# First pair of conv-norm statistics as split products behind the output products, with a new order table

## The chip, the cores and the metric

The kernel runs on one core of a Trainium2 chip. The metric is the time of one execution on the device in microseconds. TensorE is called PE here, VectorE DVE, ScalarE ACT, GpSimd POOL, and SyncE (which issues most transfers) SP. The trace is that of one profiled execution; its times count from the start of its span.

## The reference

One decoder layer over 2048 positions of width 1024: RMS norm, one input projection, a gated linear attention (GLA) on four heads, beside it a convolution of width 31 on 512 channels with a group norm, one output projection, and a feed-forward part with squared ReLU.

```python
xn = rmsnorm(h, norm1_g[l])
proj = jnp.einsum('bsd,de->bse', xn, w_in[l])
...
o_gla = gla_chunked(q, k, v, log_a)
o_gla = rmsnorm(o_gla, gla_norm_g[l]).reshape(B, S, GLA_VAL) * jax.nn.silu(g)
...
u = c_in * jax.nn.sigmoid(c_gate)
u = causal_depthwise_conv(u, conv_w[l], conv_b[l])
o_conv = jax.nn.silu(channel_group_norm(u, conv_norm_g[l], conv_norm_b[l]))
mixed = jnp.concatenate([o_gla, o_conv], axis=-1)
h = h + jnp.einsum('bse,ed->bsd', mixed, w_out[l])
...
ff = jnp.square(jax.nn.relu(jnp.einsum('bsd,df->bsf', hn, w_mlp_in[l])))
h = h + jnp.einsum('bsf,fd->bsd', ff, w_mlp_out[l])
```

The change concerns `channel_group_norm`: mean and variance over groups of 64 channels at each position, then scale, gain and silu.

## The kernel before

The mixer works through four blocks of 512 positions (b = 0 to 3 in the code, blocks one to four in the text), the feed-forward part follows. Channels lie on the partitions, 128 at a time; the 512 convolution channels are four tiles j = 0 to 3, handled in two pairs. Nearly every matrix product is done in fp32 precision as three products of rounded parts (`three_products`, lines 83 to 85: high by high, high by low, low by high). A half column of the input projection is four such triples, 12 products of 128x128 by 128x512.

The convolution runs on DVE. A tap (L1724) adds one shifted and weighted copy of `u_sb` to a sum in PSUM; 31 taps make a tile, and the last tap of a tile writes the result to `y_sb`. `("taps", p, i, n)` in the table is n taps of pair p from the i-th of 62 on.

The group norm of a pair goes through the steps `cn_mean` (PE forms the group means as a product with the block matrix `mean_grp`, DVE subtracts them from `y_sb` at L2216, ACT squares), `cn_var` (PE forms the group means of the squares, ACT takes the logarithm), `cn_rstd` (ACT exponential, POOL multiplies), `cn_silu` and `cn_mixed` (ACT and POOL write the rounded part `mix_hi` and the rest `mix_lo`, which the output products read). The sums come in two forms. A plain one is a single fp32 product (L2586 for means, L2596 for variances). A split one (`mean_of`, L2271 and L2272) is two products of rounded operands, the high and the low part of the data with `mean_grp_r`; for it ACT first writes the rounded copy or square to `mix_hi` (L1615, L1606) and POOL the difference to `mix_lo` (L1169, L1179). Step `cn_split` is that preparation for the mean; for the variance it is part of `cn_mean`. Before the change the first pair (tiles 0 and 1) has plain sums in all blocks, the second pair split ones. The rows of `mix_hi` and `mix_lo` that hold split data are the ones from which the output products of the block before read, so ACT waits for those products to end first (`w_used`, `OUT_END`).

GLA goes in four chunks of 128 positions per block. For a chunk, PE forms scores in two steps (`gla_scores c 0` and `1`; L2618, L2625; the transposes L2633 of `k_end` close the first, and they wait for the state of the chunk before), DVE picks the valid ones into `probs` by masked copies (`gla_select`; L2055, L2065, L2075, L2198), PE forms the chunk's output (L2654, L2658) and DVE updates the state (`state`, L2209). POOL makes the decayed keys (`gla_decayed`), ACT the exponentials, DVE the exponents (`gla_expo`; L2175 to L2177, subtractions with both operands in SBUF).

The order of everything in the mixer is the table `ORDER`, a list of (block, step, arguments) made ahead of time by a planner. Each engine runs through this one list and does its own part of each step in that sequence, so the table fixes the order on each engine and nothing else; waits on semaphores keep data right. In the table the entries of output products `out` in block b belong to the output of block b-1. The function `cn_bank` says into which PSUM bank a sum goes.

## Time and profile before

| | us |
|---|---|
| median of 3 runs | 2024.85 |
| lowest and highest | 2024.81, 2025.76 |
| the profiled execution | 2024.25 |
| its span in the trace | 2022.2 |
| PE busy in the span | 2000.1 |
| DVE, ACT, POOL busy | 1473.9, 956.6, 445.9 |

The span is the time from the first to the last instruction that the profiler recorded; 2.05 us of the execution lie around it. The mixer takes some 780 us of it, the feed-forward part the rest. A busy share is the mean over parts with different limits, so the stretches and the waits have to be read too. Matmuls overlap in the trace: a product of 128x512 is shown as 0.39 us long while the next begins 0.23 us after it, so distances between starts are what a product costs.

### The profile page before, as it was taken

To read this page: it belongs to the slowest core of one execution; us is meant where nothing else is said; L and a number is where in the kernel's file an instruction comes from. 1 tells how busy PE (TensorE), PEld (TensorE's weight loads), DVE (VectorE), ACT (ScalarE), POOL (GpSimd) and SP (SyncE) were. 2 spreads that over 40 slices of the span, in tenths; PEclk is the share of its full clock that TensorE was granted. 3 is DMA by queue.
4 is the path that set the end of the run, shared out by engine and by line. 5 is a ranking of instruction groups with operands and counts; after the bars stand their busy time and mean duration, and the time that the engine had idled before them with its cause. 6 is when DMAs were issued, how large, how long until landed. Compare 5 with 4: busy or idle time off the path is not lost.

```text
span 2022.2 us, 27147 instructions
## 1 busy us (share of the span) xinstructions
PE 2000.1 (99%) x9898; PEld 1635.4 (81%) x9898; DVE 1473.9 (73%) x2178; ACT 956.6 (47%) x1361; POOL 445.9 (22%) x593
## 2 busy tenths in 40 slices
PE   8999999999999999999999999999999999999998
PEld 7787778787877778888888888888888888888887
DVE  3899978887878978877789777777664646545475
ACT  4456664355244563565557645554332333323253
POOL 5553475235126441000000000000020201202031
PEclk9999999999999999999999999999999999999999
DMA  6884458555555555444445433335967557565674
GB/s 227 285 289 152 139 202 295 167 168 186 198 200 191 179 208 191 162 146 144 148 163 206 153 122 127 126 121 197 376 231 266 188 203 265 181 220 185 206 239 177
DMA packets 175268, 395.76 MB, mean 196 GB/s; under 512 B 15424, under 2 KB 64672, under 8 KB 174624
## 3 DMA queue, kind: packets, MB, share of 16 engines
q1 hardware_dynamic: 154688, 317.47, 46.3%
q10 hardware_dynamic: 20448, 76.56, 10.8%
q8 instruction: 79, 1.29, 0.3%
q14 instruction: 53, 0.43, 0.1%
HBM read 301.70 MB, written 92.27 MB: 195 GB/s over the span
## 4 chain that ended last, share of the span: by engine, by line
PE 90%; DVE 6%; issue 2%; ACT 2%; POOL 0%; DMA 0%; DVEq 0%; ACTq 0%; POOLq 0%
PE acc L83 24%; PE acc L85 24%; PE acc L84 24%; PE acc L2565 3%; PE acc L2566 3%; PE acc L2567 3%; DVE acc L1724 2%; PE acc L2625 1%; PE acc L2520 1%; PE acc L2519 1%; PE acc L2521 1%; PE acc L2284 1%; ACT ring_hi L1355 1%; PE acc L2658 1%; DVE ring_sum L1869 1%
## 5 line engine op out<-in xcount | busy, mean ns | idle before, releaser
L1986 DVE TENSOR_TENSOR down_lo<-down_raw,down_hi 128x1536 fp32r<-128x1536 f32 x112 | 200.5, 1790 | 231.1 <-ACT down_hi L1441 231.1
L84 PE MATMUL acc<-down_lo,down_hi 128*128 128x512 f32 x896 | 348.5, 389 | 0.0
L83 PE MATMUL acc<-down_hi 128*128 128x512 f32 x896 | 348.5, 389 | 0.0
L85 PE MATMUL acc<-down_hi,down_lo 128*128 128x512 f32 x896 | 348.5, 389 | 0.0
L1441 ACT ACTIVATE down_hi<-down_raw 128x1536 fp32r<-128x1536 f32 x112 | 166.7, 1488 | 360.8 <-PE acc L85 192.9
L1724 DVE SCALAR_TENSOR_TENSOR acc<-u_sb,cw_col,acc 128x512 f32<-128x512 f32 x464 | 312.9, 747 | 0.3
L1355 ACT ACTIVATE ring_hi<-ring_sum 128x512 fp32r<-128x512 f32 x155 | 97.8, 631 | 250.3 <-DVE ring_sum L1869 247.9
L83 PE MATMUL acc<-xT_hi,wt 128*128 128x512 f32 x512 | 203.6, 398 | 0.7 <-ACT q_sb L1534 0.7
L1100 POOL TENSOR_TENSOR rows_a<-rows_a,second 128x512 f32<-128x512 f32 x20 | 25.3, 1296 | 803.6 <-ACT second L1449 655.5
L84 PE MATMUL acc<-xT_lo,wt 128*128 128x512 f32 x512 | 199.5, 390 | 0.0
L85 PE MATMUL acc<-xT_hi,wt 128*128 128x512 f32 x512 | 199.5, 390 | 0.0
L84 PEld LDWEIGHTS acc<-down_lo,down_hi 128*128 128x128 f32 x896 | 168.2, 188 | 35.0
L85 PEld LDWEIGHTS acc<-down_hi,down_lo 128*128 128x128 f32 x896 | 168.2, 188 | 34.9
L83 PEld LDWEIGHTS acc<-down_hi 128*128 128x128 f32 x896 | 168.2, 188 | 34.9
L1869 DVE TENSOR_TENSOR ring_sum<-raw_w 128x512 f32<-128x512 f32 x155 | 108.1, 698 | 66.3 <-PE acc L85 64.8
L83 PE MATMUL acc<-mul_hi,ring_hi 128*128 128x512 f32 x372 | 145.5, 391 | 0.4 <-issue 0.4
L85 PE MATMUL acc<-mul_hi,ring_lo 128*128 128x512 f32 x372 | 144.8, 389 | 0.0
L84 PE MATMUL acc<-mul_lo,ring_hi 128*128 128x512 f32 x372 | 144.8, 389 | 0.0
L1878 DVE TENSOR_TENSOR ring_lo<-ring_sum,ring_hi 128x512 fp32r<-128x512 f32 x155 | 107.2, 692 | 18.4 <-ACT ring_hi L1355 3.8
L83 PEld LDWEIGHTS acc<-xT_hi,wt 128*128 128x128 f32 x512 | 96.2, 188 | 23.2 <-issue 2.2
L85 PEld LDWEIGHTS acc<-xT_hi,wt 128*128 128x128 f32 x512 | 96.1, 188 | 20.6
L84 PEld LDWEIGHTS acc<-xT_lo,wt 128*128 128x128 f32 x512 | 96.2, 188 | 20.5 <-issue 1.2
(304 smaller groups left out, 4113.2 us busy)
## 6 DMA issues: line engine op xcount, KB each, us to landing
wt<-w_kept SPq DMA_DIRECT2D x168, 512.0 KB, 3.3
down_raw<-f_kept ACTq DMA_DIRECT2D x109, 512.0 KB, 4.3
raw_w<-in_w_mlp_in SPq DMA_DIRECT2D x32, 1024.0 KB, 5.9
f_kept<-f_tile SPq DMA_DIRECT2D x128, 256.0 KB, 2.0
down_raw<-in_w_mlp_out SPq DMA_DIRECT2D x64, 512.0 KB, 3.6
w_kept<-wt SPq DMA_DIRECT2D x48, 512.0 KB, 5.3
down_raw<-in_w_mlp_out SPq DMA_DIRECT2D x64, 256.0 KB, 3.2
down_more<-f_kept ACTq DMA_DIRECT2D x29, 512.0 KB, 5.3
```

Source lines behind the costliest of these rows:

```text
L83: nc.tensor.matmul(out, w_hi, x_hi, start=first, stop=False, skip_group_check=onto)
L84: nc.tensor.matmul(out, w_hi, x_lo, start=False, stop=False, skip_group_check=onto)
L85: return nc.tensor.matmul(out, w_lo, x_hi, start=False, stop=last, skip_group_check=onto)
L1355: nc.scalar.activation(blocks(ring_hi[:, j % RING, :]), src, ACT.Copy).then_inc(a_hi, 1)
L1441: nc.scalar.activation(down_hi[d % RING][:, :], down_raw[d % DOWN_RAW][:, 512:2048], ACT.Copy).then_inc(d_hi, 1)
L1724: nc.vector.scalar_tensor_tensor(out=y_sb[:, j, :] if k == TAPS - 1 else bank, in0=u_sb[:, j, k:k + BLK], scalar=cw_col[:, j, k:k + 1], in ...
L1869: nc.vector.tensor_tensor(blocks(ring_sum[:, j % RING, :]), w1_block(w, a), w1_block(w, b), op).then_inc(a_sum, 1)
L1878: nc.vector.tensor_tensor(blocks(ring_lo[:, slot, :]), src, blocks(ring_hi[:, slot, :].bitcast(F32)), ALU.subtract).then_inc(a_lo, 1)
L1986: nc.vector.tensor_tensor(down_lo[slot][:, :], down_raw[d % DOWN_RAW][:, 512:], down_hi[slot][:, :].bitcast(F32), ALU.subtract).then_inc(d ...
L2565: nc.tensor.matmul(out, mix_hi[:, k, c], w_hi[:, slot, :], start=(k == 0), stop=False)
L2566: nc.tensor.matmul(out, mix_hi[:, k, c], w_lo[:, slot, :], start=False, stop=False)
L2567: ins = nc.tensor.matmul(out, mix_lo[:, k, c], w_hi[:, slot, :], start=False, stop=(k == KT - 1))
```

## The change

For the first pair in blocks one to three, mean and variance become split sums like those of the second pair. ACT's rounded copies and squares and POOL's differences come on, in steps `(b, cn_split, 0)` and `(b, cn_mean, 0)`. Since they use the rows of `mix_hi` and `mix_lo`, `cn_mean 0` of blocks two and three now stands behind the output products of the block before (it waits for `sum_ok`) and uses banks 4 and 5; ACT waits only for the first pair's taps. Block four keeps its plain first pair. The count of split parts gets a function of its own, `nth_part`, and one wait of a residual load and one of the output are kept for the last block alone. The table `ORDER` is made anew throughout, with the planner told of a mutual exclusion of DVE and POOL in SBUF; `make_wz`, which splits a small weight, is now its first entry.

```diff
@@ -92,152 +92,161 @@
-    (-1, "make_masks", 0), (0, "x_load", 0), (-1, "conv_gate_a", 0), (-1, "make_masks", 1), (-1, "conv_gate", 0),
...
+    (-1, "make_wz"), (-1, "make_masks", 0), (0, "x_load", 0), (-1, "conv_gate_a", 0), (-1, "conv_gate", 0),
...
@@ -625,9 +634,19 @@
 
         def cn_bank(b, j):
 
-            if b == NB - 1 and j >= 2:
-                return Y_BANK[j % 2]
-            return j if j < 2 and not first(b) else 4 + j % 2
+            if b == NB - 1:
+                return j if j < 2 else Y_BANK[j % 2]
+            return 4 + j % 2
+
+        def in_parts(b, step):
+
+            return b < NB - 1 or step[1] == 1
+
+        def nth_part(b, name, j):
+
+            if b == NB - 1:
+                return b * 2 * CT + (2 if name == "cn_mean" else 0) + j - 2 + 1
+            return (b * 2 + j // 2) * CT + (2 if name == "cn_mean" else 0) + j % 2 + 1
 
         def pair(step):
 
@@ -794,7 +813,8 @@
                 elif half == 0:
 
                     sp.wait_ge(cn_f, (m + 1) * CT)
-                    sp.wait_ge(cn_n, (m + 1) * CT + 2)
+                    if m + 1 == NB - 1:
+                        sp.wait_ge(cn_n, (m + 1) * CT + 2)
                 else:
                     sp.wait_ge(h_st, (m * 2 + half + 1) * 16)
                 sp.dma_start(res(m, half)[:, :, :], tok(x_t, m, half)).then_inc(res_ld[half], 16)
@@ -1165,7 +1185,7 @@
                     pass
                 elif name == "cn_split" and b < NB - 1:
                     for j in pair(step):
-                        pool.wait_ge(cn_part_hi, b * CT + j - 1)
+                        pool.wait_ge(cn_part_hi, nth_part(b, name, j))
                         nc.gpsimd.tensor_tensor(mix_lo[:, HEADS + j, :], y_sb[:, j, :],
                                                 mix_hi[:, HEADS + j, :].bitcast(F32), ALU.subtract).then_inc(cn_part_lo, 1)
                 elif name == "gn_square" and b < NB - 1:
@@ -1173,9 +1193,9 @@
                         pool.wait_ge(gn_sq, 2 * (b * HEADS + h + 1))
                         nc.gpsimd.tensor_tensor(mix_lo[:, h, :], gn_r[:, h, :], mix_hi[:, h, :].bitcast(F32),
                                                 ALU.subtract).then_inc(gn_sq_lo, 1)
-                elif name == "cn_mean" and step[1] == 1 and b < NB - 1:
+                elif name == "cn_mean" and b < NB - 1:
                     for j in pair(step):
-                        pool.wait_ge(cn_part_hi, b * CT + j + 1)
+                        pool.wait_ge(cn_part_hi, nth_part(b, name, j))
                         nc.gpsimd.tensor_tensor(mix_lo[:, HEADS + j, :], cn_work(j),
                                                 mix_hi[:, HEADS + j, :].bitcast(F32), ALU.subtract).then_inc(cn_part_lo, 1)
                 elif name == "cn_rstd":
@@ -1597,12 +1617,14 @@
                 elif name == "cn_mean":
                     if first(b) and step[1] == 0:
                         act.wait_ge(xt_pe, 2 * 2 * TT)
-                    if b - 2 + step[1] >= 0:
-                        act.wait_ge(h_st, ((b - 1 + step[1]) * 2 + 1) * 16)
+                    if b == NB - 1 and step[1] == 0:
+                        act.wait_ge(h_st, ((b - 1) * 2 + 1) * 16)
+                    elif not first(b):
+                        act.wait_ge(h_st, (b * 2 + 1) * 16)
                     for j in pair(step):
                         act.wait_ge(cn_dev, b * CT + j + 1)
                         nc.scalar.activation(cn_work(j), y_sb[:, j, :], ACT.Square).then_inc(cn_sq, 1)
-                        if step[1] == 1:
+                        if in_parts(b, step):
                             nc.scalar.activation(mix_hi[:, HEADS + j, :], y_sb[:, j, :],
                                                  ACT.Square).then_inc(cn_part_hi, 1)
                 elif name == "cn_split":
@@ -1610,7 +1632,7 @@
                         act.wait_ge(w_used, base(b) + OUT_END)
                     else:
                         act.wait_ge(v_st, 2 * KT * 16)
-                    act.wait_ge(tap_ok, (b + 1) * ALL_TAPS)
+                    act.wait_ge(tap_ok, b * ALL_TAPS + (step[1] + 1) * PAIR_TAPS)
                     for j in pair(step):
                         nc.scalar.activation(mix_hi[:, HEADS + j, :], y_sb[:, j, :], ACT.Copy).then_inc(cn_part_hi, 1)
                 elif name == "cn_var":
@@ -2216,12 +2238,12 @@
                         nc.vector.tensor_tensor(y_sb[:, j, :], y_sb[:, j, :], acc[:, cn_bank(b, j), :],
                                                 ALU.subtract).then_inc(cn_dev, 1)
                     for j in pair(step) if b == NB - 1 and step[1] == 1 else ():
-                        dve.wait_ge(cn_part_hi, b * CT + j + 1)
+                        dve.wait_ge(cn_part_hi, nth_part(b, name, j))
                         nc.vector.tensor_tensor(mix_lo[:, HEADS + j, :], cn_work(j),
                                                 mix_hi[:, HEADS + j, :].bitcast(F32), ALU.subtract).then_inc(cn_part_lo, 1)
                 elif name == "cn_split" and b == NB - 1:
                     for j in pair(step):
-                        dve.wait_ge(cn_part_hi, b * CT + j - 1)
+                        dve.wait_ge(cn_part_hi, nth_part(b, name, j))
                         nc.vector.tensor_tensor(mix_lo[:, HEADS + j, :], y_sb[:, j, :],
                                                 mix_hi[:, HEADS + j, :].bitcast(F32), ALU.subtract).then_inc(cn_part_lo, 1)
                 elif b == NB - 1 and name in ("cn_rstd", "cn_mixed") and step[1] == 1:
@@ -2291,7 +2313,7 @@
                     pe.wait_ge(*((sum_ok, (NB - 1) * LOWS) if t == 0 else (low_ok, m * LOWS + 2 * t)))
                 elif t == 0 and not first(m):
                     pe.wait_ge(v_ok, m * TT)
-                    if m > 1:
+                    if m == NB:
                         pe.wait_ge(cn_ln, (m - 1) * CT + 2)
                 elif t == 1 and not first(m):
                     pe.wait_ge(silu_ok, m * HEADS)
@@ -2570,33 +2592,31 @@
                         elif k == KT - 1:
                             ins.then_inc(out_pe, 1)
                 elif name == "cn_mean":
-                    if step[1] == 0:
+                    if not in_parts(b, step):
                         pe.wait_ge(tap_ok, b * ALL_TAPS + PAIR_TAPS)
-                    if step[1] == 0 and not first(b):
                         pe.wait_ge(v_ok, (b + 1) * TT)
                     else:
                         if not first(b):
                             pe.wait_ge(sum_ok, b * LOWS)
-                        elif step[1] > 0:
+                        if step[1] > 0 and b < NB - 1:
                             pe.wait_ge(cn_ln, b * CT + 2)
-                        if b < NB - 1:
                             pe.wait_ge(u_ok, (b + 1) * 2 * CT + 2)
                     for j in pair(step):
-                        if step[1] == 0:
+                        if not in_parts(b, step):
                             nc.tensor.matmul(acc[:, cn_bank(b, j), :], mean_grp[:, :], y_sb[:, j, :], start=True,
                                              stop=True).then_inc(cn_mean_pe, 1)
                         else:
-                            pe.wait_ge(cn_part_lo, b * CT + j - 1)
+                            pe.wait_ge(cn_part_lo, nth_part(b, "cn_split", j))
                             mean_of(acc[:, cn_bank(b, j), :], mean_grp_r, HEADS + j).then_inc(cn_mean_pe, 1)
                 elif name == "cn_var":
                     pe.wait_ge(cn_dev, b * CT + 2 * step[1] + 2)
                     for j in pair(step):
-                        if step[1] == 0:
+                        if not in_parts(b, step):
                             pe.wait_ge(cn_sq, b * CT + j + 1)
                             nc.tensor.matmul(acc[:, cn_bank(b, j), :], mean_grp[:, :], cn_work(j), start=True,
                                              stop=True).then_inc(cn_var_pe, 1)
                         else:
-                            pe.wait_ge(cn_part_lo, b * CT + j + 1)
+                            pe.wait_ge(cn_part_lo, nth_part(b, "cn_mean", j))
                             mean_of(acc[:, cn_bank(b, j), :], mean_grp_r, HEADS + j).then_inc(cn_var_pe, 1)
                 elif name == "gla_scores":
                     c, part = step[1:]
```

On PE in block two, the first pair's mean before the change (rows of the trace's program, in sequence; `q_in` and `qe_head` are GLA operands). Before:

```order
L2618 MATMUL acc<-qe_head,ke 64x128 [waits gn_ln,o_ok,qe_ok]
L2618 MATMUL acc<-qe_head,ke 64x128
L2625 MATMUL acc<-qe_head,ke 64x64 x8
L2633 MATMUL acc<-ident,k_end 128x128 [waits state_ok]
L2633 MATMUL acc<-ident,k_end 128x128
L2586 MATMUL acc<-y_sb,mean_grp 128x512 [waits v_ok,tap_ok]
L2586 MATMUL acc<-y_sb,mean_grp 128x512
L83 MATMUL acc<-xT_hi,wt 128x512 [waits w_again2,v_ok]
```

and after, where the product ahead of it is the last one of the first conv_gate column (`sum_ok` counts the output tiles of the block before):

```order
L83 MATMUL acc<-xT_hi,wt 128x512
L84 MATMUL acc<-xT_lo,wt 128x512
L85 MATMUL acc<-xT_hi,wt 128x512
L2293 MATMUL acc<-mix_hi,mean_grp_r 128x512 [waits cn_part_lo,sum_ok]
L2294 MATMUL acc<-mix_lo,mean_grp_r 128x512
L2293 MATMUL acc<-mix_hi,mean_grp_r 128x512 [waits cn_part_lo]
L2294 MATMUL acc<-mix_lo,mean_grp_r 128x512
L83 MATMUL acc<-xT_hi,wt 128x512 [waits w_again2,sum_ok]
```

The mean went from a place among the first chunk's scores, ahead of the output products, to one behind them, and each of the two plain products became two rounded ones.

On DVE in block one, around the masked copies of the third chunk (`probs`). Before:

```order
L2055 COPY_PREDICATED probs<-lvl_mask,acc 128x4x64 [waits probs_ok,o_pe,score_pe]
L2065 COPY_PREDICATED probs<-lvl_mask,acc 128x8x32 [waits probs_ok]
L1724 SCALAR_TENSOR_TENSOR acc<-u_sb,cw_col,acc 128x512 [waits tap_ok]
L1724 SCALAR_TENSOR_TENSOR y_sb<-u_sb,cw_col,acc 128x512 [waits tap_ok] x2
L2065 COPY_PREDICATED probs<-lvl_mask,acc 128x16x16 [waits probs_ok,score_pe]
L2085 COPY u_sb<-u_sb 128x30 [waits tap_ok]
L2089 TENSOR_TENSOR u_sb<-acc,sig 128x512 [waits u_ok,csig_ok,w_used]
L1719 TENSOR_SCALAR acc<-u_sb,cw_col,cb_col 128x512 [waits tap_ok,u_ok] x2
```

and after:

```order
L1746 SCALAR_TENSOR_TENSOR y_sb<-u_sb,cw_col,acc 128x512 [waits tap_ok] x2
L2107 COPY u_sb<-u_sb 128x30 [waits tap_ok]
L2111 TENSOR_TENSOR u_sb<-acc,sig 128x512 [waits u_ok,csig_ok,w_used]
L2077 COPY_PREDICATED probs<-lvl_mask,acc 128x4x64 [waits probs_ok,o_pe,score_pe]
L2087 COPY_PREDICATED probs<-lvl_mask,acc 128x8x32 [waits probs_ok]
L2087 COPY_PREDICATED probs<-lvl_mask,acc 128x16x16 [waits probs_ok,score_pe]
L2197 TENSOR_TENSOR fac<-cum 128x2x64 [waits ke_ok]
```

The taps that end the second pair (`y_sb`) and the product that makes `u_sb` now stand ahead of the masked copies, and the third masked copy follows the second one directly.

On DVE in block one, from the third chunk's last masked copy to the state update behind its output. Before:

```order
L2198 COPY_PREDICATED probs<-ident,acc 128x512 [waits upd_pe,probs_ok]
L2216 TENSOR_TENSOR y_sb<-y_sb,acc 128x512 [waits cn_mean_pe] x2
L1724 SCALAR_TENSOR_TENSOR acc<-u_sb,cw_col,acc 128x512 [waits tap_ok] x10
L2101 TENSOR_TENSOR z_parts<-acc,z_parts 32x512 [waits z_ok]
L1724 SCALAR_TENSOR_TENSOR acc<-u_sb,cw_col,acc 128x512 [waits tap_ok] x6
L2209 SCALAR_TENSOR_TENSOR state<-state,decay,acc 64x128 [waits state_ok,o_ok,upd_pe]
L2209 SCALAR_TENSOR_TENSOR state<-state,decay,acc 64x128 x3
L2111 TENSOR_SCALAR cum<-acc,bg_col 128x512 [waits fac_ok,gate_act]
L2055 COPY_PREDICATED probs<-lvl_mask,acc 128x4x64 [waits probs_ok,o_pe,score_pe]
L2065 COPY_PREDICATED probs<-lvl_mask,acc 128x8x32 [waits probs_ok]
```

and after:

```order
L2220 COPY_PREDICATED probs<-ident,acc 128x512 [waits upd_pe,probs_ok]
L2107 COPY u_sb<-u_sb 128x30 [waits tap_ok]
L2111 TENSOR_TENSOR u_sb<-acc,sig 128x512 [waits u_ok,csig_ok,w_used]
L1741 TENSOR_SCALAR acc<-u_sb,cw_col,cb_col 128x512 [waits tap_ok,u_ok] x2
L1746 SCALAR_TENSOR_TENSOR acc<-u_sb,cw_col,acc 128x512 [waits tap_ok] x6
L2123 TENSOR_TENSOR z_parts<-acc,z_parts 32x512 [waits z_ok]
L2231 SCALAR_TENSOR_TENSOR state<-state,decay,acc 64x128 [waits state_ok,o_ok,upd_pe]
L2231 SCALAR_TENSOR_TENSOR state<-state,decay,acc 64x128 x3
L1746 SCALAR_TENSOR_TENSOR acc<-u_sb,cw_col,acc 128x512 [waits tap_ok] x8
L2077 COPY_PREDICATED probs<-lvl_mask,acc 128x4x64 [waits probs_ok,o_pe,score_pe]
```

Between the last copy and the state update there were 16 taps and the subtraction of two means; now there are the product for `u_sb`, the two first taps and six more.

## Rows read from the trace of the kernel before

**Rows 1.** Page, part 1: busy us (share of span) and instructions of engines.

```profile
PE 2000.1 (99%) x9898; PEld 1635.4 (81%) x9898; DVE 1473.9 (73%) x2178; ACT 956.6 (47%) x1361; POOL 445.9 (22%) x593
```

**Rows 2.** Stretches: window in us, its length, then as the header row says.

```profile
core 0: us, PE busy (x) PEld busy (x) DVE busy (x) ACT busy (x) POOL busy (x), PEclk, DMA share, GB/s
...
100.00:200.00 100.00, 97.91 (x621) 77.75 (x620) 95.55 (x201) 55.89 (x79) 44.60 (x74) 1.00 0.68 227
...
600.00:700.00 100.00, 97.78 (x578) 78.28 (x578) 86.31 (x180) 53.98 (x79) 47.56 (x73) 1.00 0.53 179
...
800.00:2022.00 1222.00, 1214.52 (x5388) 1005.12 (x5386) 825.02 (x991) 553.73 (x752) 93.86 (x96) 1.00 0.55 189
```

**Rows 3.** Waits of PE: what waited, for whom, us in total, times, longest.

```profile
PE acc L2625 <- DVE probs L2065: 1.8, 2, 1.3
...
PE acc L2654 <- DVE probs L2198: 1.2, 1, 1.2
PE acc L2633 <- DVE state L2209: 1.2, 1, 1.2
PE acc L2640 <- ACT k_endT L1586: 1.1, 1, 1.1
PE acc L2674 <- DVE state L2209: 1.0, 1, 1.0
```

**Rows 4.** Timeline of PE, a plain pair: start us, us, line, operation.

```profile
155.46 1.88 PE L2586 MATMUL acc<-y_sb,mean_grp 128*128 128x512 f32 x4
156.78 0.80 PE L83 MATMUL acc<-xT_hi,wt 128*128 128x512 f32 x1
157.42 0.39 PE L84 MATMUL acc<-xT_lo,wt 128*128 128x512 f32 x1
```

**Rows 5.** Timeline of PE, a split pair and the product behind it.

```profile
194.90 0.40 PE L2271 MATMUL acc<-mix_hi,mean_grp_r 128*128 128x512 f32 x1
...
195.84 0.39 PE L2486 MATMUL acc<-xT_hi,wz 128*32 128x512 f32 x1
```

**Rows 6.** Groups of PE by line: busy us, mean ns of one record.

```profile
L2596 PE MATMUL acc<-res_sb,mean_grp 128*128 128x512 f32 x16 | 7.7, 605 | 0.0
L2586 PE MATMUL acc<-y_sb,mean_grp 128*128 128x512 f32 x16 | 7.5, 592 | 0.0
```

**Rows 7.** Timeline of PE, block one: idle time before and who ended it.

```profile
187.33 1.15 PE L2625 MATMUL acc<-qe_head,ke 128*64 128x64 f32 x32 [1.29 <-DVE probs L2065]
...
212.17 0.44 PE L2633 MATMUL acc<-ident,k_end 128*128 128x128 f32 x2 [1.16 <-DVE state L2209]
...
214.30 0.51 PE L2625 MATMUL acc<-qe_head,ke 128*64 128x64 f32 x10 [0.51 <-DVE probs L2065]
```

**Rows 8.** Timeline of DVE at that first wait.

```profile
184.88 0.75 DVE L1724 SCALAR_TENSOR_TENSOR acc<-u_sb,cw_col,acc 128x512 f32<-128x512 f32 x1
185.53 1.40 DVE L1724 SCALAR_TENSOR_TENSOR y_sb<-u_sb,cw_col,acc 128x512 f32<-128x512 f32 x2
186.85 0.42 DVE L2065 COPY_PREDICATED probs<-lvl_mask,acc 128x256 f32<-128x256 int32 x1
```

**Rows 9.** Timeline of DVE at the second.

```profile
206.57 4.03 DVE L1724 SCALAR_TENSOR_TENSOR acc<-u_sb,cw_col,acc 128x512 f32<-128x512 f32 x6
210.63 1.48 DVE L2209 SCALAR_TENSOR_TENSOR state<-state,decay,acc 64x128 f32<-64x128 f32 x4
```

**Rows 10.** Timeline, block two: POOL, and DVE beside it.

```profile
265.22 2.60 POOL L1188 TENSOR_TENSOR mix_lo<-y_sb,mix_hi 128x512 fp32r<-128x512 f32 x2 [0.69 <-ACT mix_hi L1637]
...
266.59 1.38 DVE L2176 TENSOR_TENSOR fac<-cum 128x128 f32<-128x128 f32 x1
267.89 0.28 DVE L2175 TENSOR_TENSOR fac<-cum 128x128 f32<-128x128 f32 x1
```

**Rows 11.** One tile each: ns of one, least, median, most; first and last start.

```profile
L1615 ACT ACTIVATE mix_hi<-y_sb x8: 613/624/630, 187.0 to 734.9; 128x512 fp32r<-128x512 f32 x8
...
L1169 POOL TENSOR_TENSOR mix_lo<-y_sb,mix_hi x6: 1272/1292/1297, 187.7 to 567.8; 128x512 fp32r<-128x512 f32 x6
```

295 lines of the change are left out of this document (152 added, 143 removed).

## The prediction, made before the changed kernel ran

> **What bounds the kernel now.** I read the engines' busy times first [rows 1]. TensorE (PE) is busy for 2000.1 us of a span of 2022.2 us; VectorE (DVE) comes next with 1473.9 us, GpSimd (POOL) has 445.9 us. A busy PE is not a PE at its peak, so the second view is the one by stretches [rows 2]. From 800 us to the end, the feed-forward part that the change does not touch, PE is busy for 1214.5 of 1222 us at a granted clock of 1.00. Whatever the mixer (0 to some 780 us) saves on PE therefore moves the whole later part forward, microsecond for microsecond: nothing else there is near a limit (DVE 825.0, POOL 93.9 us). In the mixer PE is also nearly full (97.9 us of 100 in one stretch shown, 97.8 in another), but DVE is full beside it in the first block: 95.6 us of 100 between 100 and 200 us, against 86.3 between 600 and 700 us. So there are two currencies: PE's own work, which counts in full, and the short times in which PE waits for DVE or ScalarE (ACT). The third view, PE's waits [rows 3], says how large the second one is: the five longest lines that lie in the mixer hold 1.8, 1.2, 1.2, 1.1 and 1.0 us, 6.3 us together. That is all there is to win from a better order on these lines; the rest must come from PE's work.
>
> **What the change removes and adds on PE.** In blocks one to three (b = 0, 1, 2) two means and two variances per block were plain fp32 products. Each is one instruction that leaves two records in the trace, so the two sums of one step stand as x4. A pair of them begins at 155.46 us, and the second of the products behind it begins at 157.42 us [rows 4]. Products of this size begin 0.23 us apart (156.78 is the modelled start of the product in between, which overlaps the last plain one), so the pair took 157.42 - 155.46 - 0.23 = 1.73 us. The split form is two rounded products for each sum; its pair, four products, begins at 194.90 us and the next work begins at 195.84 us: 0.94 us [rows 5]. The difference is 0.79 us a pair. The trace groups count 16 and 16 records of plain products, 592 and 605 ns each [rows 6], which is four pairs of means and four of variances; the last block keeps its two, so six pairs change: 6 x 0.79 = **4.8 us less work on PE**. Bounds: if only the time up to the modelled start of the next product were the pair's own (156.78 - 155.46 = 1.32 us), it would be 6 x 0.38 = 2.3 us; by the busy times (4 x 0.6 against four products 0.23 apart plus a tail) it would be at most some 5.5 us. I take 4.8, since start to start is what the engine can't give away.
>
> **What it adds elsewhere.** ACT gets, per block, two copies and two squares with rounded output, 0.62 us for a copy [rows 11] and as much taken for a square: 12 instructions, 7.5 us, on an engine that is busy for 56 and 54 us of 100 in the mixer's stretches [rows 2]. POOL gets 12 subtractions of 1.29 us [rows 11], 15.5 us, and it is busy for 45 and 48 of 100. I cost both at nothing for the end time, as long as the sums are not asked for early. The cover is the distance in PE's order. The longest new chain is at block two: the ACT copy can start only when the last output product of the block before is done (it writes the rows of mix_hi that those products read), then 0.62 us ACT and 1.29 us POOL, 1.9 us to the first part and 3.2 us to the second. On PE, scores and two half columns of conv_gate (24 products, 5.4 us) stand between the last output product and the first sum. So the sum has its operands some 3 us early; in block three the distance is longer still. The variance chain (subtract on DVE 0.7, four squares on ACT 2.5, two subtractions on POOL 2.6, 5.8 us) has ten half columns of 2.7 us of PE work to cover it in block two, and three and a chunk's output, some 10 us, in block three. Behind the waiting POOL instructions stand the decayed keys of the fourth chunk; these wait for the third chunk's scores anyway, which PE reaches some 13 us after the sum. If that cover were gone, each sum would stop PE for up to 3 us.
>
> **What it moves.** The last taps of a block's first pair of channel tiles had to be done before the pair's mean, and in blocks two and three that mean came ahead of all output products. Now it comes behind them. DVE gets over 40 us more for those taps (16 half columns of output, 12 products 0.23 us apart each), and the new table uses this: work on which PE waits goes ahead of taps. The two places that the waits name are in block one [rows 7]. At 187.33 us the second scores of the third chunk had waited 1.29 us for a masked copy of DVE; DVE was still in the last three taps (184.88 and 185.53, ending at 186.9) and reached the copy at 186.85 [rows 8]. In the new order this copy stands directly behind the first two, with no tap between. At 212.17 us the transposes of the fourth chunk had waited 1.16 us for the state of the third, which DVE began at 210.63 after six taps that began at 206.57 [rows 9], and the scores behind them another 0.51 us. PE had 12 products between the chunk's output and those scores; now it has 24 and the variance's four, 3.6 us more. These three waits, 1.29 + 1.16 + 0.51 = 3.0 us, should go. What is late next? DVE is still the fuller engine in block one, and the table also rearranges the rest of it, which the trace of before can't show. I bound what new waits cost from below by nothing and from above by the lines of rows 3: as much as all that is there now, 6.3 us, once more. I take one new wait of the longest kind [rows 7], 1.3 us, since in blocks two to four DVE has more room than in block one [rows 2]. Net: 3.0 - 1.3 = **1.7 us less waiting**, with ends at 6.3 us less and 6.3 - 3.0 = 3.3 us more.
>
> **The sum.** The profiled execution took 2024.25 us (span 2022.2 and 2.05 around it); the median of three runs is 2024.85 us, 0.6 above it. 2024.25 - 4.8 - 1.7 = 2017.75 us, and with the 0.6 us the median comes to about **2018.4 us**.
>
> **A rule weighed.** While POOL ran two subtractions from 265.22 us on, a DVE subtraction with both inputs in SBUF, which takes 0.28 us elsewhere in its series, took 1.38 us and ended as POOL's second one ended [rows 10]. The Trainium skill (SBUF — State Buffer, "Who interferes with whom") says so too: a Vector instruction with two SBUF inputs and a GpSimd instruction that reads SBUF take one shared read interface in turn, and the later of the two is blocked for the whole of the other. By that rule, the trace agrees, the change is a risk: every added POOL instruction reads two SBUF tensors. It is the rival of the other side, below.
>
> **The rivals.** (1) *The order's waits don't shrink.* The old waits go and new ones of the same size or more take their place: PE's saving stands alone or is eaten. 2024.85 - 4.8 + 0 to 3.3 us = 2020.1 to 2023.4 us, with a tail beyond it if several new waits are longer than any of the old. For it: two tables made by a planner share hardly a place after the first block, and 6.3 us of waits were left by the last one. Against it: the two longest go by construction. (2) *DVE's relief reaches further.* All of the 6.3 us goes: 2024.85 - 4.8 - 6.3 = 2013.8 us. For it: later mean, fewer deadlines for taps in blocks two and three; against it: the waits at 1.2 us (chunk output), 1.1 (k_endT) and 1.0 (group norm) are on places that the change doesn't address [rows 3]. (3) *Slower: POOL holds DVE.* Each of the 12 new POOL subtractions can hold one DVE instruction with two SBUF inputs for 1.38 - 0.28 = 1.1 us [rows 10], 13.2 us in all; if all of it reached PE, 2024.85 - 4.8 + 13.2 = 2033.3 us. It ends slower than before by more than 0.2% from 8.9 us on, that is if at least 8 of the 12 fall on work that PE is about to ask for. Against it: most of DVE's instructions are taps, which read one SBUF and one PSUM operand and went on undisturbed, and the table was made knowing of it. (4) *It doesn't do what it says.* The plain pair's tail overlapped the products behind it, and only 2.3 us go: 2022.5 us with waits as they are.
>
> **How the numbers follow.** The forecast (2017 to 2020.5 us) has 0.50; rival 1 has 0.25, rival 2 has 0.15, rival 3 has 0.06, rival 4 has 0.04. A measurement of this kernel can tell some 0.2% (4.05 us) from no change. Faster than that means below 2020.8 us: the forecast nearly whole, rival 2, and the near end of rival 1: 0.66. Within it, 2020.8 to 2028.9: most of rival 1, rival 4 and a little of the forecast: 0.27. Slower: rival 3 and the far tail of rival 1: 0.07. The range of 8 in 10 runs from rival 2's 2013.8 to the middle of rival 1: 2013.5 to 2023.5 us.
>
> **What the new profile would show.** Right: groups of plain mean_grp products with 4 and 4 records instead of 16 and 16, and 28 and 28 of the rounded ones; a pair of sums in blocks one to three 0.94 us long; PE busy some 5 us less; no wait of PE for a masked copy between the third chunk's two scores; the feed-forward part as long as before (its start 6 to 7 us earlier); POOL up by 15 us, ACT by 7. Wrong: PE waiting for POOL's mix_lo or ACT's mix_hi at a sum; PE's waits in sum above 6.3 us in the mixer, for DVE above all, with the saving in PE's work as told; DVE's two-input subtractions with mean times well above 0.3 us.

## The result

The changed kernel takes 2010.09 us (median of 4 runs, 2009.62 to 2010.24), the kernel before 2024.83 us in the same session. The ratio is 0.9928 (95% interval 0.9916 to 0.994): 14.7 us faster, where 6.4 were forecast. The direction was right and the time lies below the range given.

The profiled execution took 2010.11 us and its span is 2008.4 us, 13.8 less than before. The page's line on the engines (as [rows 1]: busy us, share of the span, instructions):

```profile
PE 1994.0 (99%) x9898; PEld 1636.2 (81%) x9898; DVE 1476.4 (74%) x2178; ACT 956.6 (48%) x1369; POOL 463.5 (23%) x605
```

PE is busy 6.1 us less than in [rows 1]. The rest of the 13.8 is time in which PE did nothing: 2022.2 - 2000.1 = 22.1 us before, 2008.4 - 1994.0 = 14.4 us now, 7.7 less. That is the first reading: the work shrank about as told, and the waits shrank by more than all that the prediction counted as waits. One sign of the prediction did not come: ACT's busy time is the same 956.6 us and not 7 up. In the new order ACT loads a function table (`ACT_TABLE_LOAD`) 52 times instead of 56 (1.28 us each, 5.1 us less), which nearly pays for the 12 new instructions. The stretches of the new trace, in the columns of [rows 2]:

```profile
core 0: us, PE busy (x) PEld busy (x) DVE busy (x) ACT busy (x) POOL busy (x), PEclk, DMA share, GB/s
...
100.00:200.00 100.00, 98.74 (x641) 79.62 (x640) 96.68 (x199) 49.13 (x75) 53.22 (x85) 1.00 0.68 227
200.00:300.00 100.00, 99.95 (x629) 81.50 (x628) 93.35 (x176) 68.89 (x106) 63.95 (x76) 1.00 0.58 200
...
600.00:700.00 100.00, 100.00 (x641) 81.04 (x640) 93.79 (x192) 49.48 (x74) 49.54 (x85) 1.00 0.58 200
```

```profile
786.00:2008.00 1222.00, 1214.83 (x5388) 1005.48 (x5386) 825.55 (x992) 553.43 (x752) 93.90 (x96) 1.00 0.55 189
```

The last 1222 us are as before (1214.8 us of PE against 1214.5), and they begin some 14 us earlier. In the mixer, stretches stand at 100.0 in which 97.8 stood, although DVE is fuller there than it was (93.8 against 86.3 between 600 and 700 us). The two windows do not hold quite the same steps, since the kernels are some 10 us apart there, but they point one way: PE's idle time in the mixer did not come from DVE's load as such, but from where the load stood.

The waits of PE (what waited, for whom, us in total, times, longest); further lines of the start and of the feed-forward part are left out:

```profile
PE acc L2714 <- POOL one_col L1001: 1.6, 1, 1.6
PE acc L2306 <- DVE x_nat L1762: 1.3, 1, 1.3
PE acc L2306 <- ACT silu_g L1570: 1.1, 1, 1.1
...
PE acc L2694 <- ACT fac L1674: 0.4, 1, 0.4
```

The first two belong to the start. None of the five lines of [rows 3] is left at its size; there is one new wait of over 1 us in the mixer, for ACT. And here are lines of the view of before that stand below those five, which the prediction did not count (the mixer, too):

```profile
PE acc L2284 <- DVE xT_lo L1756: 0.8, 1, 0.8
PE acc L2565 <- issue: 0.7, 1, 0.7
PE acc L83 <- ACT q_sb L1534: 0.7, 1, 0.7
...
PE acc L2495 <- DVE cum L2111: 0.4, 1, 0.4
```

The groups of the sums, by line (busy us, mean ns of one record), and a split pair of block one in PE's timeline:

```profile
L2293 PE MATMUL acc<-mix_hi,mean_grp_r 128*128 128x512 f32 x28 | 11.7, 418 | 0.0
...
L2294 PE MATMUL acc<-mix_lo,mean_grp_r 128*128 128x512 f32 x28 | 11.1, 396 | 0.0
...
L2616 PE MATMUL acc<-res_sb,mean_grp 128*128 128x512 f32 x4 | 1.9, 593 | 0.0
L2606 PE MATMUL acc<-y_sb,mean_grp 128*128 128x512 f32 x4 | 1.9, 592 | 0.0
```

```profile
207.00 0.40 PE L2293 MATMUL acc<-mix_hi,mean_grp_r 128*128 128x512 f32 x1
...
207.70 0.40 PE L2294 MATMUL acc<-mix_lo,mean_grp_r 128*128 128x512 f32 x1
```

16 and 16 plain records [rows 6] have become 4 and 4, the last block's. Four products begin 0.23 us apart, 0.93 us for a pair. At the place of the second wait of [rows 7], DVE now does the state (six taps stand ahead of it), then eight taps, and PE's transposes come when the state is long done (DVE, then PE):

```profile
200.66 1.48 DVE L2231 SCALAR_TENSOR_TENSOR state<-state,decay,acc 64x128 f32<-64x128 f32 x4
202.18 5.36 DVE L1746 SCALAR_TENSOR_TENSOR acc<-u_sb,cw_col,acc 128x512 f32<-128x512 f32 x8
```

```profile
203.71 0.44 PE L2653 MATMUL acc<-ident,k_end 128*128 128x128 f32 x2
```

### The profile page after: what moved, and what is told of

Read it like the earlier page. It is cut to its first block, busy times and chain, and to the rows that moved or that the text cites. A ratio compares the mean times of both kernels' runs of the same rounds, so it can differ in the third digit from the quotient of the medians.

```text
span 2008.4 us, 27171 instructions
## 1 busy us (share of the span) xinstructions
PE 1994.0 (99%) x9898; PEld 1636.2 (81%) x9898; DVE 1476.4 (74%) x2178; ACT 956.6 (48%) x1369; POOL 463.5 (23%) x605
## 3 DMA queue, kind: packets, MB, share of 16 engines
q8 instruction: 79, 1.29, 0.3%
## 4 chain that ended last, share of the span: by engine, by line
PE 90%; DVE 6%; ACT 2%; issue 1%; DMA 1%; DVEq 0%; SPq 0%; ACTq 0%; POOL 0%; POOLq 0%
PE acc L83 24%; PE acc L84 24%; PE acc L85 24%; PE acc L2587 3%; PE acc L2588 3%; PE acc L2589 3%; DVE acc L1746 2%; PE acc L2645 1%; PE acc L2542 1%; PE acc L2541 1%; PE acc L2543 1%; PE acc L2306 1%; ACT ring_hi L1375 1%; PE acc L2678 1%; DVE ring_sum L1891 1%
## 5 line engine op out<-in xcount | busy, mean ns | idle before, releaser
L1375 ACT ACTIVATE ring_hi<-ring_sum 128x512 fp32r<-128x512 f32 x155 | 97.8, 631 | 249.7 <-DVE ring_sum L1891 247.1
```

The lines of the kernel that those rows point to most:

```text
L1375: nc.scalar.activation(blocks(ring_hi[:, j % RING, :]), src, ACT.Copy).then_inc(a_hi, 1)
```

## The experiments

Theory A: the split products are worth 4.8 us of PE's work, and all the rest is waits that the new table took away, the two adding up. Rivals: PE's work was sized too small (B); split products and order only work together (C); POOL's holds cost something (D). Each kernel was timed in five rounds (4 to 11 executions) against the kernel before, whose median was 2024.3 to 2024.7 us in these sessions. "Idle" is the span less PE's busy time in its profiled execution. It is not all time that a better order could win: where PE ran at the lower of its two levels, time that was lost stands as busy (last section).

| run | what it is | us | ratio, 95% interval | PE busy | idle |
|---|---|---|---|---|---|
| before | | 2024.83 | | 2000.1 | 22.1 |
| changed | | 2010.09 | 0.9928, 0.9916 to 0.994 | 1994.0 | 14.4 |
| e1 | new table, plain products | 2014.53 | 0.9952, 0.9939 to 0.9966 | 1999.6 | 12.9 |
| e2 | new table, plain sums | 2015.01 | 0.9954, 0.9941 to 0.9966 | 1999.6 | 13.3 |
| e3 | old table, split sums | 2041.30 | 1.0085, 1.0071 to 1.0098 | 2004.0 | 35.3 |
| e4 | before, three entries moved | 2029.17 | 1.0022, 1.0013 to 1.0031 | 2004.6 | 22.4 |
| e5 | before, taps put off | 2027.47 | 1.0016, 1.0007 to 1.0025 | 2001.8 | 23.3 |
| e6 | new table, early mean | 2032.38 | 1.0042, 1.0029 to 1.0054 | 2001.5 | 27.3 |
| e7 | new block one, old rest | 2028.97 | 1.002, 1.0011 to 1.0029 | 2003.0 | 24.8 |
| e8 | old block one, new rest | 2019.46 | 0.9975, 0.9966 to 0.9985 | 1999.2 | 18.5 |
| e9 | e5 with late mean, late taps | 2029.13 | 1.0022, 1.0013 to 1.0031 | 2003.1 | 24.1 |
| e10 | before with late mean | 2030.60 | 1.0027, 1.0017 to 1.0038 | 2003.5 | 25.2 |
| e11 | changed, POOL's part twice | 2015.31 | 0.9952, 0.994 to 0.9965 | 1996.5 | 16.9 |
| e12 | changed, one entry moved | 2010.99 | 0.9935, 0.9921 to 0.9948 | 1994.1 | 14.8 |

### The two halves of the change (e1 to e3)

e1 lets PE compute the first pair's sums as plain products at the places of the new table; ACT's and POOL's preparation stays.

```diff
                     for j in pair(step):
-                        if not in_parts(b, step):
+                        if step[1] == 0:
+                            if b < NB - 1:
+                                pe.wait_ge(cn_part_lo, nth_part(b, "cn_split", j))
                             nc.tensor.matmul(acc[:, cn_bank(b, j), :], mean_grp[:, :], y_sb[:, j, :], start=True,
...
-                        if not in_parts(b, step):
+                        if step[1] == 0:
+                            if b < NB - 1:
+                                pe.wait_ge(cn_part_lo, nth_part(b, "cn_mean", j))
                             pe.wait_ge(cn_sq, b * CT + j + 1)
```

> The changed kernel with its new table, in which PE computes the first pair's means and variances of blocks one to three as plain fp32 products again, at the same places; the rounded copies and squares of ACT and the differences of POOL stay, but nobody reads them. It measures PE's part of the gain alone. Theory A (PE's work counts 0.79 us a pair, the rest of the gain is waits that the new table took away): 2010.1 + 4.8 = 2014.9 us, and PE's stalls as in the changed kernel. Theory B (PE's work is the larger part and was sized too small, up to 2.4 us a pair): 2020 us or more. Theory C (the order found now only fits the split products): over 2017 us, with new stalls of PE.

Measured: 2014.53 us, 4.4 above the changed kernel, which was timed in another session; against the kernel before of each session the two gain 9.8 and 14.7 us, 5.0 apart. Theory A's 4.8 holds within this and B falls. No stall of PE is new against the changed kernel; what rose is its busy time, by 5.6 us. Of these, 1.2 lie in the first 70 us, where PE ran at its lower level for a while in e1's profiled execution (see e2), and 4.4 behind them.

e2 takes the preparation out, too: the old code in the new table.

```diff
-            return b < NB - 1 or step[1] == 1
+            return step[1] == 1
...
-                elif name == "cn_mean" and b < NB - 1:
+                elif name == "cn_mean" and step[1] == 1 and b < NB - 1:
...
-    (0, "cn_split", 0), (1, "cn_split", 0), (2, "cn_split", 0)
```

> As the run with plain products in the new table, and the 12 copies and squares of ACT and the 12 differences of POOL are left out as well: the code of before in the table of after. Theory A, by which these instructions cost nothing: the same 2014.9 us, within 1 us of that run. Theory D (POOL holds DVE in SBUF, 1.1 us for each of the 12, and some of it reaches PE): lower than that run by 3 to 13 us, about 2005 to 2012 us. Against the kernel before, this run is what the new table is worth alone: by theory A 2024.8 - 2014.9 = 9.9 us.

Measured: 2015.01 us. Without the 24 instructions on ACT and POOL it is not faster than e1 (0.5 us slower, within the runs' spread), so D's 3 to 13 us fall, and the split as a whole is worth 4.9 us. The traces say why: of the 240 two-input subtractions of DVE for the exponents, five take over 0.8 us in the kernel before, in the changed one, in e1 and in e2 alike, so the added POOL instructions brought no further hold there. Against before, the new table alone is worth 9.3 us (2024.3 - 2015.0). The mixer behind the start, before and e2 (columns as [rows 2]):

```profile
70.00:800.00 730.00, 720.77 (x4214) 577.28 (x4213) 618.76 (x1145) 371.54 (x555) 315.59 (x437) 1.00 0.59 201
```

```profile
70.00:800.00 730.00, 727.77 (x4254) 585.26 (x4254) 629.38 (x1152) 369.47 (x555) 320.80 (x444) 1.00 0.59 203
```

PE's idle time there falls from 9.2 to 2.2 us: 7.0 of the 9.3. By the table above it would be 22.1 - 13.3 = 8.8, but 1.7 of these are no gain: in e2's profiled execution PE ran at a granted clock of 0.72 between 8 and 14 us and was busy for longer in the start, while block one's first product with `xT_hi` and `wt` begins at 36.1 us in both kernels. The other 2.3 us of the 9.3 stand as busy time. A part of them is how waits are shown: the trace counts a wait from the modelled end of a product, 0.16 us behind the point where the next one could have begun (0.39 - 0.23), and the mixer has 14 waits before and 6 in e2, which as an estimate makes 1.3 us. No run takes the rest apart.

e3 is the other half: split sums in the old table, with only their own steps moved.

```diff
-(0, "taps", 1, 30, 3), (0, "cn_mean", 0), (0, "conv_in_a", 1)
+(0, "gla_decayed", 2, 2), (0, "cn_split", 0), (0, "taps", 1, 59, 3), (0, "gla_select", 2, 1), (0, "conv_gate", 2), (0, "cn_mean", 0)
+(0, "gla_scores", 2, 0), (0, "cn_var", 0), (0, "cn_rstd", 0)
...
+(1, "gla_decayed", 3, 2), (1, "cn_split", 0)
+(1, "conv_in", 0), (1, "cn_mean", 0)
+(1, "conv_gate", 1), (1, "cn_var", 0), (1, "cn_rstd", 0)
...
+(2, "gla_decayed", 3, 2), (2, "cn_split", 0)
+(2, "conv_gate", 1), (2, "cn_mean", 0)
+(2, "conv_gate", 2), (2, "cn_var", 0), (2, "cn_rstd", 0)
```

> The other half alone: the split products of the first pair in the table of before, in which only that pair's own steps moved (in blocks two and three behind the output products, where the split form can stand; in block one behind the second column of conv_in, since the rows of mix_hi hold other data until then). Theory A: 2024.8 - 4.8 = 2020.0 us, plus up to 3 us for places chosen by hand. Theory C (split and order belong together, the later mean gives DVE its relief at once): 2016 us or less. If the split form holds other engines up (theory D): over 2024 us.

Measured: 2041.30 us, and the expectation fails by 21 us. Its waits of PE, the two longest lines (L1181 is the difference for the mean, L1191 the one for the variance), and the longest single one with what DVE, ACT and POOL did ahead of it:

```profile
PE acc L2285 <- POOL mix_lo L1191: 6.6, 2, 6.2
PE acc L2285 <- POOL mix_lo L1181: 5.9, 4, 2.8
```

```profile
190.91 0.77 PE L2285 MATMUL acc<-mix_hi,mean_grp_r 128*128 128x512 f32 x1 [6.23 <-POOL mix_lo L1191]
```

```profile
187.49 1.28 DVE L2230 TENSOR_TENSOR y_sb<-y_sb,acc 128x512 f32<-128x512 f32 x2
```

```profile
188.26 0.63 ACT L1618 ACTIVATE res_sb<-y_sb 128x512 f32<-128x512 f32 x1 [14.20 <-DVE y_sb L2230]
```

```profile
189.49 2.52 POOL L1191 TENSOR_TENSOR mix_lo<-res_sb,mix_hi 128x512 fp32r<-128x512 f32 x2 [13.85 <-ACT mix_hi L1620]
```

PE waits 12.5 us for POOL's parts, but POOL is only the last link. In the longest wait it had been idle for 13.85 us, and ACT for 14.20: both waited for DVE's subtraction of the mean, which came at 187.49 us, behind 13 taps, the masked copies and three taps more. So here, too, it is DVE's taps that stand ahead of what PE asks for, and a held DVE instruction (D) is not in this chain, though the time lies where D's "over 2024 us" had it. The waits are not all of the loss: PE's lower level costs some 7 us more (last section). Split sums cost other engines nothing only where the table puts them far enough behind their preparation. This is C in its plain meaning: the split needs a table made for it, while the table (e2) gains without the split.

### Where in the table the gain lies (e7, e8)

Both have plain sums; one table is used up to the first product of block two's values, from there on the steps of the other that are still to do, in its order.

```diff
-ORDER = before
+ORDER = new[: new.index((1, "v", 0))] + [e for e in before if e not in those]
```

> Plain sums; the new table up to the products of the values of block two, from there on the table of before. Where the table's 9.3 us lie: PE's stalls of before up to that place add up to some 5.9 us and 4.6 in the start, of the changed kernel to 1.9 and 4.1. Expected: 2024.3 - 4.4 = 2019.9 us. If the gain is not in places but in the order as a whole (what is saved early is lost at the seam or later): 2022 us or more.

```diff
-ORDER = before
+ORDER = before[: before.index((1, "v", 0))] + [e for e in new if e not in those]
```

> Plain sums; the table of before up to the products of the values of block two, from there on the new one. PE's stalls of before behind that place add up to 5.4 us in the mixer, of the changed kernel to 1.1: 2024.3 - 4.3 = 2020.0 us, and with the run of the other half together the 9.3 us. If the gain is one of block one, where DVE is fuller: 2023 us or more.

Measured: e8 2019.46 us, 4.9 less than before, near the 4.3 expected. e7 2028.97 us, 4.6 more than before, where 4.4 less were expected. But e2, which has both halves, is 4.4 us below e8. So the new block one gains 4.4 us in front of the new rest and loses 4.6 in front of the old one. e7's waits of PE name the place, and DVE's row for the last of block two's exponents the cause; in the kernel before that row begins at 244.71 us (shown with e5 below):

```profile
PE acc L2621 <- ACT qe_head L1583: 5.9, 2, 5.7
```

```profile
250.72 0.41 DVE L2180 TENSOR_TENSOR fac<-cum 128x256 f32<-128x256 f32 x1
```

The new block one leaves taps undone. Counted in the tables, 147 taps stand ahead of the first product of block two's values in the new one, 162 in the old one. In e7 the 15 missing ones stand ahead of the exponents of block two. These end 6.0 us later, then come POOL's decayed keys and ACT's copies, and PE's first scores wait 5.7 us. PE is at its lower level behind that wait, for another 2 us of loss.

### Waits repaired by hand (e4, e5)

e4 moves the three entries that the prediction's three waits name.

```diff
-(0, "taps", 1, 59, 3), (0, "gla_select", 2, 1)
+(0, "gla_select", 2, 1), (0, "taps", 1, 59, 3)
...
-(1, "taps", 0, 12, 6), (0, "gla_out", 2), (0, "gla_heads", 3), (1, "gate", 0), (1, "qk_a", 1), (0, "gla_select", 3, 0), (0, "gla_select", 3, 1)
+(0, "gla_out", 2), (0, "gla_heads", 3), (1, "gate", 0), (1, "qk_a", 1), (0, "gla_select", 3, 0), (0, "gla_select", 3, 1), (1, "taps", 0, 12, 6)
```

> The kernel before with three entries moved and nothing else: the masked copy of the third chunk ahead of the three taps, and the six taps between the third chunk's output and the fourth one's masked copies behind these. They are the three waits of 1.29, 1.16 and 0.51 us that the prediction named. If they go and nothing is late in their place: 2024.8 - 3.0 = 2021.8 us. If the taps that were put back are what the next wait is for: 2023.5 to 2025 us.

Measured: 2029.17 us, 4.9 slower. The waits of [rows 7] are gone, and two longer ones stand behind them (PE's timeline, with ACT's row between):

```profile
189.89 0.40 PE L2640 MATMUL acc<-head_cols,qk 128*64 128x2 f32 x8 [1.94 <-ACT k_endT L1586]
...
227.28 0.71 PE L2654 MATMUL acc<-q_in,state 64*128 64x128 f32 x8 [3.24 <-DVE probs L2198]
```

```profile
188.42 1.15 ACT L1615 ACTIVATE mix_hi<-y_sb 128x512 fp32r<-128x512 f32 x2 [8.40 <-DVE y_sb L1724]
```

The taps that made way finish the second pair. On ACT the rounded copies of that pair (`cn_split 1`) stand ahead of the `k_endT` copy, so ACT waits for the taps and PE for ACT, longer than PE had waited for the masked copy. And the six taps, put back behind the second masked copy of the fourth chunk, came ahead of its last copy, for which PE waits 3.24 us. PE's idle time in the mixer grew by 2.5 us in all; some 1.7 us more went to PE's lower level behind the first of the two (last section), and 0.9 us lie in the start of this profiled execution, which no entry here touches.

e5 repairs by amount instead.

```diff
-(1, "x_sq", 1), (0, "cn_split", 1), (0, "gla_scores", 2, 0)
+(1, "x_sq", 1), (0, "gla_scores", 2, 0), (0, "cn_split", 1)
...
-taps of pair 0, block two: 12 ahead of step z, 18 ahead of (0, "gla_out", 2), 25 ahead of (0, "gla_out", 3)
+taps of pair 0, block two: 8 ahead of (0, "gla_out", 2), 16 ahead of (0, "gla_out", 3), 9 behind (0, "gn_square")
```

> The run with three moved entries lost 4.9 us: ACT's copy of the last taps stood ahead of the copy on which PE then waited 1.94 us, and the taps put back made PE wait 3.24 us for the last masked copy. This run is the kernel before with the same repair done by amount of work: the third chunk's masked copy ahead of the three taps, step cn_split 1 behind the third chunk's first scores, and DVE has done as many taps when PE asks for the third and the fourth chunk's output as in the changed kernel (132 and 140 instead of 142 and 149); nine taps go behind the fourth one. Theory E (the waits in block one are DVE's taps ahead of PE's demand, whoever orders them): the three waits go and nothing of their size comes, 2024.3 - 3.0 = 2021.3 us. Rival F (waits are tied to the whole order, hand repair always finds the next): 2024 us or more.

Measured: 2027.47 us. The waits in block one shrink (1.29, 1.16 and 0.51 us go or fall below 0.2, two of 0.8 and 0.6 us come), but in block two PE waits longer than anywhere in the kernel before. PE, ACT and DVE of e5, and the last row of the same exponents in the kernel before:

```profile
263.11 0.54 PE L2618 MATMUL acc<-qe_head,ke 128*64 128x128 f32 x3 [3.30 <-ACT qe_head L1580]
```

```profile
261.15 1.91 ACT L1580 ACTIVATE qe_head<-qe 64x896 f32<-64x896 f32 x2
```

```profile
248.28 0.41 DVE L2177 TENSOR_TENSOR fac<-cum 128x256 f32<-128x256 f32 x1
```

```profile
244.71 0.42 DVE L2177 TENSOR_TENSOR fac<-cum 128x256 f32<-128x256 f32 x1
```

The exponents end 3.6 us later, PE waits 3.3 us, and behind that wait it runs at its lower level, 1.7 us of loss: the whole rise of its busy time in the table. The taps put off are a debt, and in the old order of block two it falls due ahead of the exponents.

### Does the late mean carry the debt? (e6, e9, e10)

e6 puts the first pair's statistics of blocks two and three back ahead of the output products, in the new table.

```diff
-(1, "conv_gate", 0), (1, "gla_expo", 3), (1, "cn_mean", 0)
+(1, "g_a", 3), (1, "taps", 0, 61, 1), (1, "cn_mean", 0)
+(1, "g", 3), (1, "cn_var", 0), (1, "x_tr", 0)
...
+(2, "gla_scores", 0, 1), (2, "cn_mean", 0)
+(2, "g", 3), (2, "cn_var", 0), (2, "x_tr", 0)
```

> The new table with plain sums, with mean, variance and power of the first pair put back ahead of the output products in blocks two and three, where the kernel before has them; its code and its PSUM banks. It tests the prediction's reason for the relief in those blocks (the later mean lets taps be put off). If the later mean was the source: the 4 to 5 us won there are gone, 2019 to 2020 us. If it was only a better search (in both tables the taps of the first pair are done well ahead of the output products): 2015 us, plus up to 2 us where the variance's chain is asked for too early at places chosen by hand.

Measured: 2032.38 us, 17 more than e2. Two of PE's waits in block two, one behind the other:

```profile
282.71 1.94 PE L2293 MATMUL acc<-ident,x_nat 128*128 128x128 f32 x16 [2.15 <-ACT res_sb L1628]
306.77 1.15 PE L2634 MATMUL acc<-qe_head,ke 128*64 128x64 f32 x32 [2.56 <-DVE probs L2074]
```

The first is the variance's chain, on whose banks the transposes wait: the last tap of the first pair stands behind 71 half columns and other weight units in the new table and behind 66 in the old one (124 and 118 in block three), and there is no room left for mean and variance ahead of the output products. So the new table does use the late mean. In block three PE waits three times more for over 2 us, and its lower level adds 2.4 us. Since places chosen by hand cost something of their own (e3, e10), I do not take the 17 us as its worth.

e10 and e9 make a cross with before and e5. e10 has the old table with the late mean and no tap moved; e9 has e5's block one, the late mean, and in block two the taps as late as the new table has them.

```diff
-(1, "cn_mean", 0), (1, "cn_var", 0), (1, "cn_rstd", 0) ahead of the output products
+(1, "conv_in", 0), (1, "cn_mean", 0)
+(1, "conv_gate", 1), (1, "cn_var", 0), (1, "cn_rstd", 0)
...
+(2, "conv_gate", 1), (2, "cn_mean", 0)
+(2, "conv_in", 1), (2, "cn_var", 0), (2, "cn_rstd", 0)
```

> Plain sums in the table of before, in which only mean, variance, power and silu of the first pair of blocks two and three moved: behind the output products, as in the changed kernel, with its PSUM banks. No tap moved. If the late place by itself frees DVE or PE: 2021 us or less. By the reading that it only gives leave to put taps off: no change, 2024.3 us, plus up to 2 us for places chosen by hand.

```diff
 as e10 and e5, and
-(1, "taps", 0, 25, 11) ahead of (1, "v", 0), the rest up to 61 ahead of (1, "gla_select", 0, 0)
+(1, "taps", 0, 23, 3) behind (1, "v", 2)
+(1, "taps", 0, 26, 24) behind (1, "gla_factors", 0)
+(1, "taps", 0, 50, 6) ahead of (1, "g_a", 0)
+(1, "taps", 0, 56, 5) ahead of (1, "g_a", 2)
+(1, "taps", 0, 61, 1) behind (1, "gla_select", 0, 2)
```

> The run with the late mean alone, and the order of block one of the run with fewer taps, but the taps that it puts off are now done as late as in the changed kernel: 147 of all taps ahead of the first product of the values instead of 162, the last tap of the first pair five half columns later. In the run with fewer taps they stood ahead of the exponents of block two, and PE waited 3.3 us for the operands of its first scores. Theory G (taps put off in block one pay only if they may be late in block two as well, which takes the late mean): the 3.3 us go and the three waits stay away, 2021.3 us, 3 us below the run with the late mean alone and 6 below the one with fewer taps. Rival F (only an order that is searched as a whole gains): 2024 us or more.

Measured: e10 2030.60, e9 2029.13 us. Neither beats before, and e9's 2021.3 failed. They end 5.9 and 4.4 us above before, and most of that lies in block three, where PE waits for POOL's part of a group norm sum and then runs at its lower level (1.7 us of loss in e10, 1.4 in e9). In e10 POOL waits for ACT there, which had the squares and the silu of the moved pair first, with two table loads of 1.28 us. e10's waits:

```profile
PE acc L2282 <- POOL mix_lo L1183: 3.2, 2, 2.8
```

What the cross shows is the difference. With the early mean, putting taps off costs 3.1 us (2024.4 to 2027.5); with the late one it gains 1.5 (2030.6 to 2029.1). The 3.30 us wait of e5 is gone in e9. By these medians late mean and late taps are worth 4.6 us to an order that puts taps off, and the late mean alone nothing; 1.7 of the 4.6 are the loss at PE's lower level behind e5's wait. The intervals of the four ratios leave some 3 us of doubt on the 4.6, none on the 3.30 us wait. The cross is not clean, though: e9 also moves taps within block two. Of its 62 taps of the first pair, 56 still stand ahead of block two's second scores, where the early mean had its place (behind `gla_select 0 0`, in e9 only the last six taps come after it), and it is 12 taps, moved from ahead of the first chunk's exponents to behind them, that take the load off these. The early mean forbids only the last six of the 62 at their place. The old table with the early mean, the same 12 taps behind the exponents and all 62 ahead of the mean was not run, so it is not shown that it takes the late mean to remove the 3.30 us wait.

### POOL's part, and the longest wait that is left (e11, e12)

```diff
                         pool.wait_ge(cn_part_hi, nth_part(b, name, j))
+                        if step[1] == 0:
+                            nc.gpsimd.tensor_tensor(mix_lo[:, HEADS + j, :], y_sb[:, j, :],
+                                                    mix_hi[:, HEADS + j, :].bitcast(F32), ALU.subtract).then_inc(twice, 1)
+                            pool.wait_ge(twice, b * 4 + j + 1)
```

> The changed kernel, in which POOL does each of its 12 new subtractions twice (the first of the two is overwritten by the second, which waits for it). It takes POOL's share of the change by a doubled dose. Prediction's rival 3 (each such instruction can hold a DVE instruction for 1.1 us and the hold reaches PE): up to 2010.1 + 13.2 = 2023.3 us, at least 2013 us. If POOL's work lies beside and only the longer chain to a sum counts (2.6 us later, where some 3 us of cover stood): 2010.1 to 2011.5 us.

Measured: 2015.31 us, 5.2 more. Its waits and its longest one:

```profile
PE acc L2302 <- POOL mix_lo L1208: 2.7, 3, 1.8
```

```profile
205.12 0.66 PE L2302 MATMUL acc<-mix_hi,mean_grp_r 128*128 128x512 f32 x1 [1.78 <-POOL mix_lo L1208]
```

2.7 us of the 5.2 are sums that wait for their parts in blocks one and three, and 1.5 us are PE's lower level behind the wait of 1.78 us (last section); some 1 us is left that I did not trace. The time lies in the range that rival 3 had here (2013 us and more) and above the other one's 2011.5, but by these two items it is the longer chain, and not held DVE instructions, that makes most of it. So the cover is about as thin as told (some 3 us). It does not bear on D for a single helping, which e2 settles.

```diff
-(0, "gla_decayed", 1, 0), (0, "taps", 1, 9, 6), (0, "gla_heads", 0), (0, "taps", 1, 15, 1), (0, "g", 3)
+(0, "gla_decayed", 1, 0), (0, "taps", 1, 9, 7), (0, "g", 3), (0, "gla_heads", 0)
```

> The changed kernel with one entry moved, at the longest wait of PE that is left in its mixer: at 129.57 us PE waits 1.07 us for ACT's silu of the fourth g column, because ACT does the 1.92 us of qe_head copies first. The copies go behind that silu. If the wait was alone: 2010.1 - 1.07 = 2009.0 us, or 2009.5 with part of it passed on to the scores that read qe_head. By what the runs with moved entries showed (a hand move in this order finds the next wait): 2010 to 2013 us.

Measured: 2010.99 us against 2010.09, not faster. The wait of 1.07 us is gone, and two of 0.6 us stand in e12's waits for it:

```profile
PE acc L2637 <- ACT qe_head L1599: 0.6, 1, 0.6
PE acc L2305 <- DVE xT_lo L1777: 0.6, 1, 0.6
```

## Why the prediction was wrong, step by step

- **PE's work, 4.8 us less: right.** Six pairs at 0.79 us; e1 and e2 measured 4.4 and 4.9 (up to 5.5 if each is set against the kernel before of its session). The Trainium skill (FP8 and Floating Point Precision, "TensorE Precision Notes") gives a true fp32 product four passes through the array; by that, as an estimate, a pair would save four products of 0.23 us and six pairs 5.4 us. The trace agrees roughly (0.86 us for one plain product are 3.8 of them), and the measurements lie below it. Start to start was the right price, and the measurement lies between the bounds told, 2.3 and 5.5. The upper one does not follow from its own terms: 4 x 0.6 less four products 0.23 apart with a tail of 0.16 is 1.3 us a pair, 7.9 in all; a plain pair's 1.88 us [rows 4] less 0.94 would give 5.6. PE's busy time fell by 6.1 us and would have been the wrong measure: outside the start it is already 2.2 us lower with the new table and plain sums (e2), and only the next 4.3 are the split. Rival 4 fell.
- **ACT's and POOL's 24 instructions at nothing: right** (e1 against e2), and the cover named for them is real: e11 shows 1.8 us for one sum when it is cut short. In e3 one sum waits 6.2 us and not the 3 told, because the chain begins with a subtraction on DVE that stands behind taps; the 3 us counted ACT's and POOL's part alone.
- **Rival 3, POOL holds DVE: fell.** The effect is there, as in [rows 10], in the changed kernel as well. POOL's row is another of its subtractions with two SBUF inputs (`cn_mixed`); DVE's are two-input subtractions of one series:

```profile
287.33 2.65 POOL L1208 TENSOR_TENSOR mix_lo<-y_sb,mix_hi 128x512 fp32r<-128x512 f32 x2
```

```profile
287.45 1.38 DVE L2198 TENSOR_TENSOR fac<-cum 128x128 f32<-128x128 f32 x1
288.75 1.37 DVE L2197 TENSOR_TENSOR fac<-cum 128x128 f32<-128x128 f32 x1
290.05 0.28 DVE L2198 TENSOR_TENSOR fac<-cum 128x128 f32<-128x128 f32 x1
```

  By the Trainium skill's rule (SBUF — State Buffer, "Who interferes with whom") the later of the two is blocked for the whole of the other; the trace agrees, with 1.38 us where 0.28 is usual. But PE waited for none of these series. That the planner knew of the exclusion did not make the holds rarer: five of 240 before, five now. So it can't be what the gain comes from. (A slip of the rival's own: to lose 8.9 us takes nine holds of 1.1 us, not eight.)
- **Three waits gone, 3.0 us: right that they go, wrong why.** They went, but not "by construction": e4 moved those very entries and was 4.9 us slower. Moving a short instruction ahead of taps passes the delay to whoever needs the taps, or to the next copy. In the new table they go because 10 and 9 taps fewer stand ahead of the third and fourth chunk's output (132 and 140 of all taps instead of 142 and 149); e5, with just these numbers in the old table, lost the three waits as well.
- **The step that failed is the term for the waits, 1.7 us, and in it the sentence that 6.3 us together "is all there is to win".** The table won 9.3 us, 7.0 of them idle time of PE in the mixer (e2 against before). First, five lines of a view with many more were taken for the whole: four others of the mixer hold 2.6 us more. The whole was to be had from two numbers on the page, the span less PE's busy time: 22.1 us, of which 7.5 lie behind 800 us [rows 2], so up to 14.6 lay ahead of it, 5.2 of that in the first 70 us, where the table won nothing, and 9.2 in the mixer. Second, a wait of the longest kind was put back as the price of a new order; one came (1.07 us, for ACT), but in all the mixer's idle time fell from 9.2 to 2.0 us. Third, 2.3 us of the table's gain lie in what the trace shows as busy time, for which the prediction had no term.
- **The later mean as DVE's relief: the table uses it (e6), what it is worth is not shown.** It was told as 40 us of room for DVE but priced only at three places of block one. What the runs show acts across blocks: block one leaves 15 taps more to block two, which gains only if block two does them behind the exponents of its first chunk (e5, e7, e9). Whether that takes the later mean, the runs leave open: only six taps stand behind the early mean's old place in e9 and in the new table. Rival 2 had this with chance 0.15 and bounded it by the same 6.3 us, so even its 2013.8 us was 3.7 too high; it came nearest. Its "against", that three of the waits lie on places that the change does not address, was no reason: a new table addresses all places.
- **What stays open.** The 4.6 us are the size of the interplay of late mean and late taps in a hand-made order, not a share of the table's 9.3. How much a new search with the old mean would have won, and what knowing the exclusion brought, no run here tells: it takes the planner.

## What to carry to other kernels

What an order can win is about the time in which the bounding engine is idle, span less busy time over the stretch that is reordered. A list of its longest waits is a part of that, and no bound. Even the idle time is no strict one: here the table won 9.3 us out of 9.2 and left 2.2, because some lost time is shown as busy. A wait read from a full engine is a debt of that engine: moving the one instruction that is waited for hands the debt on, and only work that may truly come later (here taps behind the exponents of the next block) pays it. A deadline that moves late is therefore to be priced by the work which it lets slip past all the waits ahead of it, in the blocks before too, and by what could have slipped without it; and a hand-made order is a poor stand-in for a searched one (e3, e9, e10), so that it can refute a claim on a mechanism's sign but not size it.

## What the runs showed of the hardware that was not expected

After e4's wait of 1.94 us PE ran at its lower level for a time. Stretches of e4 (columns as [rows 2]) and two of the products in one of them:

```profile
190.00:193.00 3.00, 3.00 (x23) 2.39 (x24) 3.00 (x10) 2.97 (x4) 1.65 (x2) 0.79 0.00 0
193.00:196.50 3.50, 3.50 (x12) 2.78 (x11) 2.63 (x12) 3.46 (x5) 0.00 (x0) 0.70 0.07 12
196.50:200.00 3.50, 3.50 (x16) 2.35 (x16) 1.82 (x4) 1.71 (x2) 1.72 (x3) 1.00 0.59 202
```

```profile
192.61 0.63 PE L83 MATMUL acc<-xT_hi,wt 128*128 128x512 f32 x1
193.03 0.63 PE L84 MATMUL acc<-xT_lo,wt 128*128 128x512 f32 x1
```

Eight products begin 0.43 us apart instead of 0.23, which is 1.2 instead of 2.4 GHz and 1.6 us, nearly as much as the wait itself. The granted clock is 0.79 and 0.70 in the two stretches and 1.00 behind them. Neither the kernel before nor the changed one, e1, e2, e8 or e12 has such a stretch in its mixer; every other run has. The ones of e5 (behind its wait of 3.30 us), e11 (behind 1.78) and e10 (behind 2.80 and 0.45), in this order:

```profile
264.00:268.00 4.00, 4.00 (x14) 1.80 (x10) 2.70 (x5) 2.44 (x4) 3.95 (x4) 0.57 0.01 2
```

```profile
205.00:209.00 4.00, 3.88 (x26) 3.07 (x27) 3.90 (x7) 2.73 (x4) 2.59 (x4) 0.57 0.05 17
```

```profile
590.00:594.00 4.00, 4.00 (x12) 1.65 (x11) 0.00 (x0) 2.52 (x3) 1.90 (x2) 0.57 0.00 0
```

PE's busy time in such a stretch, times what the granted clock lacks to 1.00, is what it costs (an estimate from these rows): 1.7 us in e4, e5 and e10, 1.5 in e11, 1.4 in e9, 2.0 in e7, 2.4 in e6 and 7.3 in three stretches of e3. The length of the wait alone does not tell: e4's wait of 3.24 us and e6's of 2.15 and 2.56 us left the clock at 1.00. So a stall can cost nearly twice its length, and part of what the orders made by hand lost (e3 to e11) is this. In e4 it stands beside waits that grew from 3.0 to 5.2 us.
